# Seven block products for eight in the feed-forward up products of a fused decoder step

## The reference, cut to what matters

```python
def conv_ffn(xn, conv_prev, lp):
    h = xn @ lp['ffn_w_up']                 # 1024 -> 2 * 2816
    u, v = h[..., :D_FF], h[..., D_FF:]
    u_full = jnp.concatenate([conv_prev, u], axis=1)
    u_c = causal_dwconv(u_full, lp['ffn_conv_w'], lp['ffn_conv_b'])   # width 3
    y = (jax.nn.silu(u_c) * v) @ lp['ffn_w_down']
    return y, u_full[:, -(FFN_CONV - 1):]
```

## Time and profile before

| what | us |
|---|---|
| three runs: median (lowest to highest) | 1521.39 (1516.34 to 1524.19) |
| the profiled execution: its time | 1515.41 |
| its span on the core | 1513.6 |
| TensorE, matmul busy in the span | 1436.1 |
| VectorE, ScalarE, GpSimd busy | 708.5, 509.7, 205.8 |

### The profile page before, as it was taken

The page is one execution under the profiler, slowest core; times in us unless marked ns, Lnnn a source line. Parts: engine busy times, 40 slices in busy tenths (PEclk is TensorE's granted clock), DMA queues, the critical chain, the costliest instruction groups (busy, mean ns, idle before and its releaser), DMA issues.

```text
span 1513.6 us, 18883 instructions
## 1 busy us (share of the span) xinstructions
PE 1436.1 (95%) x6560; PEld 1030.1 (68%) x6560; DVE 708.5 (47%) x1430; ACT 509.7 (34%) x1349; POOL 205.8 (14%) x322
## 2 busy tenths in 40 slices
PE   7989789999999999999999888899999999999999
PEld 5666657777766777777776566577777667777776
DVE  1355668888324444430013456588883334444200
ACT  1236437766214111110002463377662331111000
POOL 2010232111022000001100102321111120000000
PEclk9999889999899999999999998899999999999999
DMA  7330525443135443333443305244431353443333
GB/s 257 115 113 0 192 81 134 116 111 91 31 123 172 126 123 117 122 96 133 145 127 117 96 1 192 89 128 122 110 84 57 120 177 126 125 118 120 105 115 97
DMA packets 79408, 174.95 MB, mean 116 GB/s; under 512 B 11761, under 2 KB 46098, under 8 KB 78418
## 3 DMA queue, kind: packets, MB, share of 16 engines
q1 hardware_dynamic: 75664, 164.11, 35.3%
q0 software_dynamic: 3360, 9.18, 2.0%
q10 hardware_dynamic: 290, 0.45, 0.1%
HBM read 167.41 MB, written 6.29 MB: 115 GB/s over the span
## 4 chain that ended last, share of the span: by engine, by line
PE 81%; DVE 10%; ACT 4%; issue 2%; DMA 1%; SPq 1%; DVEq 0%
PE pair L458 36%; PE pair L1053 13%; PE pair L809 6%; PE pair L810 6%; PE pair L922 4%; PE bank L843 2%; DVE small L1430 2%; PE pair L899 1%; DVE small L1409 1%; PE pair L816 1%; ACT area L1598 1%; ACT area L1590 1%; PE pair L1038 1%; DVE xg L1420 1%; PE pair L1039 1%
## 5 line engine op out<-in xcount | busy, mean ns | idle before, releaser
L458 PE MATMUL pair<-xg,slot 128*128 128x320 f32 x2048 | 559.0, 434 | 9.2 <-DMA slot<-in_weights 9.2
L458 PEld LDWEIGHTS pair<-xg,slot 128*128 128x128 f32 x2048 | 389.8, 191 | 173.8 <-DMA slot<-in_weights 9.2
L1409 DVE TENSOR_REDUCE small<-sq 128x8 f32<-128x512 f32 x256 | 168.1, 682 | 54.2 <-ACT sq L1816 53.0
L1053 PE MATMUL pair<-area,slot 128*128 128x320 f32 x704 | 189.8, 432 | 0.0
L1598 ACT ACTIVATE area<-area 128x336 f32<-128x336 f32 (+4 forms) x112 | 63.5, 567 | 334.0 <-DVE area L1547 300.8
L1053 PEld LDWEIGHTS pair<-area,slot 128*128 128x128 f32 x704 | 133.8, 190 | 55.7
L1816 ACT ACTIVATE sq<-pair 128x512 f32<-128x512 f32 x256 | 152.2, 595 | 5.2 <-DVE small L1409 5.2
L1490 DVE TENSOR_TENSOR x<-x,pair 128x320 f32<-128x320 f32 x48 | 23.4, 487 | 244.0 <-PE pair L1053 174.8
L809 PE MATMUL pair<-wkq,area 128*128 128x288 f32 x320 | 107.4, 417 | 0.5 <-DMA area<-in_cache 0.5
L810 PE MATMUL pair<-wkq,area 128*128 128x288 f32 x320 | 103.8, 406 | 0.0
L1966 POOL TENSOR_SCALAR xg<-x,par 128x320 f32<-128x320 f32 x48 | 58.5, 1226 | 262.2 <-DVE x L1490 256.7
(11 more groups left out here) (392 smaller groups left out, 1689.9 us busy)
## 6 DMA issues: line engine op xcount, KB each, us to landing
slot<-in_weights SPq DMA_DIRECT2D x216, 512.0 KB, 3.6
area<-in_cache SPq DMA_DIRECT2D x160, 130.0 KB, 2.1
kept<-in_cache SPq DMA_DIRECT2D x96, 130.0 KB, 2.1
slot<-in_weights SPq DMA_DIRECT2D x18, 384.0 KB, 4.2
xg<-in_ssd_t SPq DMA_DIRECT2D x2, 1024.0 KB, 4.8
area<-in_ssd_n SPq DMA_DIRECT2D x2, 1024.0 KB, 13.6
hs_out<-area POOLq DMA_DIRECT2D x2, 1024.0 KB, 4.1
x<-in_x SPq DMA_DIRECT2D x2, 640.0 KB, 6.1
```

What stands on the lines that cost most here:

```text
L458: last = mm(out[:, 0:T], w[:, k, :], xg[:, k, :], start=(k == 0), stop=(k == KD - 1))
L1053: last = mm(b[:, 0:T], w[j // 8][:, j % 8, :], hff[:, j, :], start=(j == 0), stop=(j == NFF - 1))
L1409: dve.tensor_reduce(ssk[:, t % 2, 8 * j:8 * j + 8], ksq[k % 3], AX.X, ALU.add).then_inc(V.fire(on["k_summed"]), 1)
```

## The change

20 of the 22 pairs of a layer no longer go through `project`. For a pair, the weights of u and v are cut into halves of the input features (u0, u1, v0, v1: 4 blocks of 128 each), and the normed tokens into the same halves and into two halves of 160 columns. u and v at both token halves would be eight products of (4 blocks) x (160 columns); Strassen's scheme in the Winograd form makes them from seven, with sums of weights and of tokens before and sums of products behind.

- Once a layer VectorE multiplies `rsx` into the tokens (`token_sums`: `xs`, two instructions of 4 x 320 columns), since sums of tokens need it ahead of the product, and makes three sums of token quarters of 640 columns; GpSimd makes the fourth.
- For each pair GpSimd makes three sums of weight halves of 512 columns (`weight_sums`), one pair ahead, and VectorE a fourth (`weight_sum`), all into two buffers.
- TensorE's `seven` makes the seven products of a pair in the order 1, 6, 5, 3, 2, 7, 4, each 4 blocks x 160 columns, in a ring of all eight banks.
- ScalarE copies products 1, 5 and 4 out of PSUM; VectorE adds up the others with them (`up_first`, `up_second`, `value_part`), and GpSimd makes v from sums (`value_sum`).
- The first two pairs stay as they were.

```diff
-                for j in range(NFF):
+                for j in range(PLAIN):
                     project(l, "fu", j, norm=3 * l + 2 if j == 0 else None)
                     project(l, "fv", j)
+                for j in range(PLAIN, NFF):
+                    seven(l, j)
```

TensorE's new function:

```diff
+            def seven(l, j):
+
+                i, w = j - PLAIN, wsum[j % 2]
+
+                def product(p, held, moving):
+                    out = banks.open("seven", "p", l, j, p)
+                    pe.wait_ge(*banks.before("p", l, j, p))
+                    for k in range(4):
+                        last = mm(out[:, 0:HALF], held[:, k, :], moving[:, k, :], start=(k == 0), stop=(k == 3))
+                    last.then_inc(banks.full("p", l, j, p), 1)
+                u = slot("fu", j, "p", l, j, 7).rearrange("p (k c) -> p k c", k=KD)
+                if i == 0:
+                    pe.wait_ge(*on["xs_ready"].at(l, 2))
+                product(1, u[:, 0:4, :], xq[0][0])
+                if i == 0:
+                    pe.wait_ge(*on["t_dve"].at(l, 3))
+                pe.wait_ge(*on["w_pool"].at(l, 3 * i + 2))
+                product(6, w[1], tsum[1])
+                pe.wait_ge(*on["w_pool"].at(l, 3 * i + 1))
+                product(5, w[0], tsum[0])
+                pe.wait_ge(*on["w_dve"].at(l, i + 1))
+                product(3, w[3], xq[1][1])
+                product(2, u[:, 4:8, :], xq[1][0])
+                if i == 0:
+                    pe.wait_ge(*on["t_pool"].at(l))
+                pe.wait_ge(*on["w_pool"].at(l, 3 * i + 3))
+                product(7, w[2], tsum[2])
+                v = slot("fv", j, "p", l, j, 4).rearrange("p (k c) -> p k c", k=KD)
+                product(4, v[:, 4:8, :], tsum[3])
```

VectorE (`up_plain`, `up_conv` and `hidden` hold the instructions that were there, `hidden` with a wait for `value_sum` ahead of its second product):

```diff
+            def weight_sum(l, j):
+                (u0, u1, u_here), _ = up_weights(l, j)
+                w = wsum[j % 2]
+                dve.wait_ge(*u_here)
+                dve.wait_ge(*on["w_pool"].at(l, 3 * (j - PLAIN) + 2))
+                if j >= PLAIN + 2:
+                    dve.wait_ge(*banks.filled("p", l, j - 2, 3))
+                TTO(w[3], u1, w[1], ALU.subtract).then_inc(V.fire(on["w_dve"]), 1)
...
+            def up_second(l, j):
+
+                u, n = ubuf[j % 2], TP - HALF
+                b = banks.of("p", l, j, 6)
+                dve.wait_ge(*V.last)
+                dve.wait_ge(*banks.filled("p", l, j, 6))
+                dve.wait_ge(*banks.emptied("p", l, j, 1))
+                TTO(sum_u2, b[:, 0:HALF], prod_a[j % 2], ALU.add).then_inc(V.free("p", l, j, 6), 1)
+                dve.wait_ge(*V.last)
+                dve.wait_ge(*banks.emptied("p", l, j, 5))
+                TTO(sum_u4, sum_u2, prod_df[j % 2][:, 1, :], ALU.add).then_inc(V.step(), 1)
+                dve.wait_ge(*V.last)
+                dve.wait_ge(*on["u_saved"].at(l, j - 1))
+                b = banks.of("p", l, j, 3)
+                dve.wait_ge(*banks.filled("p", l, j, 3))
+                TTO(u[:, 2 + HALF:2 + TP], b[:, 0:n], sum_u4[:, 0:n], ALU.add).then_inc(V.step(), 1)
+                us = u[:, 2 + TP:].rearrange("p (b c) -> p b c", b=NB)
+                TTO(us[:, :, 2:], bview(b[:, n:HALF]), bview(sum_u4[:, n:HALF]), ALU.add).then_inc(V.free("p", l, j, 3), 1)
...
+                for j in range(PLAIN, NFF):
+                    hidden(l, j - 1)
+                    up_second(l, j)
+                    if j + 1 < NFF:
+                        weight_sum(l, j + 1)
+                    up_first(l, j)
+                    up_conv(l, j)
+                    value_part(l, j)
+                hidden(l, NFF - 1)
```

`up_first` adds product 2 and the copy of product 1 into the first 160 columns of u; `value_part` adds product 7 and `sum_u2`. ScalarE, where `gate` is the sigmoid as before:

```diff
+                for j in range(PLAIN, NFF):
+                    gate(j - 1)
...
+                    copy(prod_a[j % 2], b[:, 0:HALF]).then_inc(A.free("p", l, j, 1), 1)
...
+                    for n, p in ((1, 5), (0, 4)):
+                        b = banks.of("p", l, j, p)
+                        act.wait_ge(*banks.filled("p", l, j, p))
+                        copy(prod_df[j % 2][:, n, :], b[:, 0:HALF]).then_inc(A.free("p", l, j, p), 1)
```

GpSimd:

```diff
+                def weight_sums(j):
+                    (u0, u1, u_here), (v0, v1, v_here) = up_weights(l, j)
+                    w = wsum[j % 2]
+                    if j >= PLAIN + 2:
+                        pool.wait_ge(*banks.filled("p", l, j - 2, 7))
+                    pool.wait_ge(*u_here)
+                    pool.wait_ge(*v_here)
+                    TTO(w[0], v0, v1, ALU.add).then_inc(G.fire(on["w_pool"]), 1)
+                    pool.wait_ge(*G.last)
+                    TTO(w[1], w[0], u0, ALU.subtract).then_inc(G.fire(on["w_pool"]), 1)
+                    TTO(w[2], u0, v0, ALU.subtract).then_inc(G.fire(on["w_pool"]), 1)
+
+                def value_sum(j):
+                    pool.wait_ge(*banks.emptied("p", l, j, 4))
+                    pool.wait_ge(*banks.emptied("p", l, j, 7))
+                    pool.wait_ge(*on["h_ready"].at(l, j - 1))
+                    TTO(vr[j % 2].rearrange("p (a t) -> p a t", a=2), prod_df[j % 2], spread(sum_u3[j % 2], 1, 2),
+                        ALU.add).then_inc(G.fire(on["v_sum"]), 1)
...
                 for j in range(NFF):
-                    pool.wait_ge(*banks.emptied("fu", l, j))
+                    if j == PLAIN - 1:
+                        pool.wait_ge(*on["xs_ready"].at(l, 2))
+                        TTO(tsum[2], xq[1][1], xq[0][1], ALU.subtract).then_inc(G.fire(on["t_pool"]), 1)
+                    if PLAIN <= j + 1 < NFF:
+                        weight_sums(j + 1)
+                    pool.wait_ge(*(banks.emptied("fu", l, j) if j < PLAIN else banks.emptied("p", l, j, 3)))
                     u = ubuf[j % 2]
                     pool.tensor_copy(fco[:, j, 0:2], u[:, TP:TP + 2]).then_inc(G.step(), 1)
...
                     if j + 2 < NFF:
                         edge(j + 2)
+                    if j >= PLAIN:
+                        value_sum(j)
```

More of the change, by code:

```diff
@@ L102 @@
 STORES = 10
+PLAIN, HALF = 2, T // 2
+NSEVEN = NFF - PLAIN
 class Signal:
@@ L433, in trunk, with slot_of, up_weights @@
         slot_reader = []
+        def slot_of(l, kind, i):
+            n = next(n for n, k in enumerate(SLOTS) if k[:2] == (kind, i)) + l * len(SLOTS)
+            return ring[n % NSLOT], (slot_in[n % NSLOT], 16 * (n // NSLOT + 1))
+        def up_weights(l, j):
+            out = []
+            for kind in ("fu", "fv"):
+                w, here = slot_of(l, kind, j)
+                w = w[:, :].rearrange("p (k c) -> p k c", k=KD)
+                out.append((w[:, 0:4, :], w[:, 4:8, :], here))
+            return out
         @block.tensor
@@ new lines, in value_part, with up_conv @@
+            def value_part(l, j):
+                if j >= PLAIN + 2:
+                    dve.wait_ge(*on["v_sum"].at(l, j - PLAIN - 1))
+                b = banks.of("p", l, j, 7)
+                dve.wait_ge(*banks.filled("p", l, j, 7))
+                TTO(sum_u3[j % 2], b[:, 0:HALF], sum_u2, ALU.add).then_inc(V.free("p", l, j, 7), 1)
+            def up_conv(l, j):
+                u, c = ubuf[j % 2], uc[j % 2][:, 0:UCONV]
+                dve.wait_ge(*V.last)
+                dve.wait_ge(*on["u_edge"].at(l, j + 1))
+                TSO(c, u[:, 0:UCONV], pc(l, "fc_w", j), pc(l, "fc_b", j), ALU.mult, ALU.add).then_inc(V.step(), 1)
+                dve.wait_ge(*V.last)
+                STT(c, u[:, 1:1 + UCONV], pc(l, "fc_w", NFF + j), c, ALU.mult, ALU.add).then_inc(V.step(), 1)
+                dve.wait_ge(*V.last)
+                STT(c, u[:, 2:2 + UCONV], pc(l, "fc_w", 2 * NFF + j), c, ALU.mult, ALU.add).then_inc(V.fire(on["uc_ready"]), 1)
@@ new lines, in hidden @@
+            def hidden(l, j):
+                full, v = ue[j % 2], vr[j % 2]
+                e, c = full[:, 0:UCONV], uc[j % 2][:, 0:UCONV]
+                dve.wait_ge(*on["u_sigmoid"].at(l, j + 1))
+                TTO(e, e, c, ALU.mult).then_inc(V.step(), 1)
+                dve.wait_ge(*V.last)
+                if j >= PLAIN:
+                    dve.wait_ge(*on["v_sum"].at(l, j - PLAIN + 1))
+                TTO(hff[:, j, 0:TP], e[:, 0:TP], v[:, 0:TP], ALU.mult).then_inc(V.step(), 1)
+                TTO(bview(hff[:, j, TP:T]), new_of(full), bview(v[:, TP:T]), ALU.mult).then_inc(V.fire(on["h_ready"]), 1)
@@ L1529, in mlp @@
                 dve.wait_ge(stored, 16 * (STORES * l + STORES - 1))
[L1530 to L1550, removed]
-                    if j:
[L1552 to L1559, removed]
@@ new lines, in mlp @@
+                for j in range(PLAIN):
+                    up_plain(l, j)
+                    if j == 0:
+                        token_sums(l)
+                    up_conv(l, j)
+                    b = banks.of("fv", l, j)
+                    if j == PLAIN - 1:
+                        weight_sum(l, j + 1)
+                    dve.wait_ge(*banks.filled("fv", l, j))
+                    TTO(vr[j % 2], b[:, 0:T], rsx[:, :], ALU.mult).then_inc(V.free("fv", l, j), 1)
+                    if j:
+                        hidden(l, j - 1)
```

(2 more changed lines are left out.)

55 lines of the change are left out of this document (52 added, 3 removed).

## The result

The changed kernel takes 1525.92 us (median of 20 runs, 1519.38 to 1534.04), the kernel before 1520.49 us (20 runs, 1511.56 to 1526.30): a ratio of 1.0043, with a 95% interval of 1.0022 to 1.0064. The forecast was 1492 us; the change costs 0.4% where it was to save 2%. The profiled spans are 1519.6 us after and 1513.6 before.

The account below looks back on a forecast made before the run. TensorE's records bound the kernel at 8.57 us a pair; a ring of 7.9 would replace that: (8.57 - 7.9) x 40 = 27, taken as 26 us, giving 1489 to 1495, forecast 1492; range 1478 to 1529, the forecast's own 1480 to 1507.

Parts of the forecast that it names:

- The port: Up stage: a VectorE instruction with two SBUF inputs and a GpSimd sum exclude each other throughout; the later waits.
- the ring of `hidden`, sums and taps: Up stage, VectorE, ScalarE and GpSimd in a cycle including all four GpSimd sums: 7.9 us a pair against TensorE's 7.67.
- VectorE's own ring: Up stage, taps, sigmoid, `hidden`, sums and evictions in order without port waits: 6.4 us a pair, below TensorE's 7.67.
- signs of being wrong: Up stage: sums of 512 over 1.1 us, port waits reaching the taps, or satisfied waits opening gaps between TensorE's products.
- 512 cost 0.89 plus a start of some 0.05: 0.94; 320 cost 0.61: GpSimd's new sums in each pair, priced in us by column count from its rows of 1024 and 2048 columns.
- third rival: GpSimd sums dear enough to make the kernel slower: decides from W = 1.125, 1557 us at 1.4; chance 0.17.
- W: Price of one GpSimd sum of 512 columns in the up stage: taken as 0.94 us, 1.12 by the skill page.
- the formula: Up-stage pair length when the ring sets the pace: 7.9 + 3.6 x (W - 0.94) us.
- second rival: GpSimd's two-full-operand sums eat the gain: W 1.05 to 1.2, ring 8.3 to 8.85, 1507 to 1529 us; chance 0.2.
- the layout: One up-stage pair timed from value_part's end, third weight sum after the second product of `hidden`: 7.9 us.
- four bare waits: Up-stage ring: four wait instructions that nothing covers, 0.05 us each a pair.
- a slack of a few tenths: Up stage's start, token sums delaying the first tap 5.5 us: a few tenths spare, else some 1 us a layer.

Follow-up runs that it names:

- memsets: Changed kernel with GpSimd's three weight sums replaced by memsets of 1350 columns from the third seven-product pair on: 1475.55 us.
- halves: Changed kernel with each of GpSimd's three weight sums made in two instructions of 256 columns: 1479.3 us, ratio 0.9708 to the kernel before.
- sum_forms: Kernel before, plus one unused GpSimd sum of 512 columns a pair in 16 pairs a layer, in four forms by turns: 1518.63 us.
- third_late: Changed kernel with GpSimd's third weight sum waiting until the second product of `hidden` is done, from the third seven-product pair on: 1520.21 us.
- repeated run: Changed kernel with the second operand of GpSimd's three weight sums made four columns repeated 128 times each: 1512.42 us.

## Why the prediction was wrong

**TensorE: right.** 56 records a pair at 0.136 (0.137 predicted), 7.61 us a pair where nothing else holds it up, for 7.67; and the old pair is 8.61, for 8.57. The gain was there to be had, 1.00 a pair for the 0.90 predicted: memsets and halves show it.

**Mechanism: right.** The port, held for the whole length of a GpSimd sum, makes the ring of `hidden`, sums and taps set the pace; VectorE's own ring is 6.4 as laid out. In the steady state the taps were not reached (0.46, 0.57, 0.57 as before); in the second pair of a layer, beside GpSimd's token sum and first weight sums, they were (1.06, 1.45 and 1.28 from 491.74 on), one of the prediction's signs of being wrong. TensorE doesn't wait for it in the first layer, and loses at most 0.8 us by it in the second (under "first pairs").

**The step that failed: "512 cost 0.89 plus a start of some 0.05: 0.94; 320 cost 0.61".** The measured prices are 1.27 and 0.87. The row that I chose is the same operation, but with one operand repeated along the columns, which accounts for 0.23, and read without most of its start, which accounts for 0.10 (sum_forms); two full operands were not in the trace. The sum of 320 columns has a repeated operand too, but repeated as a whole block of 160 columns, and it costs 0.87 where a start of 0.17 and 1.70 ns a column (from 1.04 and 1.91) would give 0.71, an estimate. The rival named just this ("two full operands cost more than one full and one repeated") and the third rival's bound was W = 1.125; at 1.27 the formula gives 7.9 + 3.6 x 0.33 = 9.1, and 8.95 was measured. So the ring passed TensorE's old pace, the point from which the third rival decides, and TensorE waits in each pair for w[1] and for a bank, as that rival had it. The prediction's own sign of being wrong, sums over 1.1 us, came true. The time is on the wrong side, but stayed near the top of the second rival's 1507 to 1529, for the reason under "first pairs" below. The Trainium skill's figure ("GPSIMD Engine Reference", §3.1), from which I estimated 1.12, lay nearer than my row, though below the measured 1.27 too.

**How the 1.04 us of the ring divide.** By the table: +0.58 ahead of e*c, of which the value sum's price is 0.26 and the first sum's 0.33; nothing at the second sum, which begins 0.29 us before e*c ends and still takes only 1.23; +0.65 at the third, of which third_late gives back 0.27 as order alone: the layout had the second product slip in ahead of the third sum, but GpSimd, told of nothing, began at once. The four bare waits that I added (0.20) weren't there. The agreement of 9.1 with 8.95 is thus partly luck: the formula counts 0.33 for the second sum, which the ring doesn't feel, and 0.20 of waits that weren't there, and the order that I had laid out wrongly, some 0.3, makes up for much of it. The repeated run shows it: with 1.04 for 1.27 the pair is 8.44, not the 8.25 expected.

**The first pairs softened it.** At 8.95 for 8.61, 20 pairs would have lost 6.8 us a layer. 2.9 and 3.8 were lost, because TensorE runs the first three seven-product pairs of a layer at or near 7.61 before it has to wait for sum_u2 in each pair. From the first of the seven products (494.87 and 1245.93) to the first down product the 20 pairs take 175.1 us in the first layer and 176.0 in the second, 3.9 and 3.0 less than 20 x 8.95 = 179.0. The second layer gains less because of the stage's start, where the prediction saw a slack of a few tenths and else some 1 us: there TensorE's third product starts 0.8 us late, since it waits for a bank that VectorE, late behind the token sums and the blocked taps, empties with the v of the second pair (L1685). VectorE's lag at the end of the stage is then hidden by the down products, as predicted (L1117 waits 0.6 us in all). The prediction had set the lag of the first pairs against the stage's start and taken 1 us off the gain for both (26 for 27).

## What to carry to other kernels

Price an operation of GpSimd by a row with the same operands, full or repeated, and not only the same name; where the trace has none, the break-even price should carry the chance. When GpSimd reads SBUF beside a VectorE chain that has two SBUF inputs, count each sum as a stop of the chain for about its whole length, and lay out which instruction meets it if neither engine is told to wait. Cutting such a sum into halves cost GpSimd a little more time (2 x 0.67 for 1.27) but returned the whole gain here (a ratio of 0.971); cutting on, into quarters, gave most of it back (0.989), because GpSimd's starts then fill its time: 128 columns take 0.45, so four take 1.8 where 512 in one take 1.27.

## What the runs showed of the hardware that was not expected

A second operand repeated along the columns makes a GpSimd sum of 512 columns 0.23 us shorter (1.04 for 1.27), while add, subtract and multiply of full operands agree within 3 ns.

A blocked sum seems to take its start while it waits: the second sum ends 0.94 us after e*c does, though a sum alone takes 1.27, and the sum of 1024 columns ends 1.77 after the instruction that blocked it, though it takes 1.91 with the port free. That it is the start which is hidden is read from these differences; no run separates it.

The same instructions ahead of the up stage run at two granted clocks in different executions. Windows and timeline of TensorE, third_late first, the changed kernel second (the window's clock is the third number from the end):

```profile
400.00:450.00 50.00, 49.02 (x232) 39.68 (x232) 10.26 (x20) 5.54 (x11) 10.84 (x9) 0.86 0.29 95
...
413.52 33.43 PE L954 MATMUL pair<-mix,slot 128*128 128x64 f32 x128
```

```profile
400.00:450.00 50.00, 48.81 (x254) 37.86 (x254) 11.19 (x22) 7.20 (x15) 10.85 (x9) 1.00 0.32 105
...
412.99 27.11 PE L954 MATMUL pair<-mix,slot 128*128 128x64 f32 x128
```

The same 128 records (80 of 320 columns and 48 of 64; the row carries only one of the shapes) take 33.43 us where the clock was at 1.2 GHz for part of the stretch and 27.11 where it stayed at 2.4; TensorE had waited 0.98 us for VectorE 2 us earlier in both. Of the twelve kernels' profiles six show the longer time and six the shorter. The kernel before is one of the former (0.86 from 400 to 450) and the changed kernel one of the latter, which other stretches make up for (0.97 and 0.86 from 200 to 250); in the up stage, where the change is, the clock is 1.00 in both. What decides between the two was not tried. It is 6.3 us, as much as the effect under study, and the reason why lone times are read here only beside the length of a pair.
